# The down stage of eight feed-forward blocks: its units in another order

## What is computed

```python
def swiglu(h, w1, w3, w2):
    return (jax.nn.silu(h @ w1) * (h @ w3)) @ w2
# x = x + 0.5 * swiglu(rmsnorm(x, g), w1, w3, w2)   D = 1024, D_FF = 2816
```

## Time and profile before

| | us |
|---|---|
| median of 3 runs | 2255.55 |
| lowest, highest | 2254.95, 2256.36 |
| the profiled execution, its own time | 2255.33 |
| its span, first to last instruction | 2253.5 |
| TensorE busy | 2226.4 (99%) |
| TensorE weight loads | 1890.5 (84%) |
| VectorE busy | 1711.6 (76%) |
| ScalarE busy | 1305.8 (58%) |
| granted TensorE clock, mean | 1.000 (2.4 GHz) |
| DMA | 467.92 MB, 208 GB/s on average |

### The profile page before, as it was taken

One profiled execution on the slowest core, in us unless ns is written; L12 is line 12 of the kernel. 1 busy time (PEld: TensorE's weight loads), 2 busy tenths in 40 slices (PEclk: granted clock), 3 DMA queues, 4 the chain that ended last, 5 costly groups with the idle time before them and its releaser, 6 DMA issues.

```text
span 2253.5 us, 28616 instructions
## 1 busy us (share of the span) xinstructions
PE 2226.4 (99%) x11542; PEld 1890.5 (84%) x11542; DVE 1711.6 (76%) x2067; ACT 1305.8 (58%) x1425; POOL 42.2 (2%) x52
## 2 busy tenths in 40 slices
PE   9999999999999999999999999999999999999999
PEld 8888888888887888887888888888888878888887
DVE  7876567868878566877887799768788777976876
ACT  7655445555655544655655676455565557754654
POOL 0000000000000000000000000000000000000000
PEclk9999999999999999999999999999999999999999
DMA  7876455767758455577576753547667575345756
GB/s 264 261 225 245 168 191 181 249 199 229 233 181 278 171 178 196 200 226 237 206 245 213 235 171 128 205 157 244 216 225 238 169 254 200 107 168 196 232 181 204
DMA packets 171859, 467.92 MB, mean 208 GB/s; under 512 B 18608, under 2 KB 22576, under 8 KB 171728
## 3 DMA queue, kind: packets, MB, share of 16 engines
q1 hardware_dynamic: 164672, 428.35, 53.8%
q0 software_dynamic: 6912, 37.75, 9.3%
q10 hardware_dynamic: 144, 0.00, 0.0%
HBM read 464.99 MB, written 1.05 MB: 207 GB/s over the span
## 4 chain that ended last, share of the span: by engine, by line
PE 87%; DVE 9%; DMA 2%; ACT 1%; issue 0%; SPq 0%; DVEq 0%; ACTq 0%
PE psum L771 25%; PE psum L772 13%; PE psum L707 12%; PE psum L709 12%; PE psum L708 12%; DVE split_w L1851 4%; PE psum L782 3%; PE psum L739 2%; PE psum L790 2%; DVE split_w L1858 1%; DVE x L2048 1%; DVE late_sums L1867 1%; PE psum L900 1%; PE psum L904 1%; PE psum L902 1%; DMA raw<-ffn_w_down_alone_dram 1%
## 5 line engine op out<-in xcount | busy, mean ns | idle before, releaser
L1851 DVE TENSOR_TENSOR split_w<-raw,split_w 128x2048 fp32r<-128x2048 f32 (+2 forms) x405 | 854.1, 2118 | 179.6 <-ACT split_w L1328 177.6
L771 PE MATMUL psum<-xt,split_w 128*128 128x512 f32 x2464 | 858.7, 393 | 0.5 <-DVE split_w L1851 0.5
L1328 ACT ACTIVATE split_w<-raw 128x2048 fp32r<-128x2048 f32 (+2 forms) x405 | 716.7, 1778 | 204.6 <-PE psum L709 95.2
L772 PE MATMUL psum<-xt,split_w 128*128 128x256 f32 x2464 | 688.1, 279 | 0.0
L771 PEld LDWEIGHTS psum<-xt,split_w 128*128 128x128 f32 x2464 | 461.3, 187 | 105.2 <-DVE split_w L1851 2.2
L772 PEld LDWEIGHTS psum<-xt,split_w 128*128 128x128 f32 x2464 | 464.9, 189 | 0.3
L707 PE MATMUL psum<-split_w,xt 128*128 128x512 f32 (+1 forms) x736 | 289.5, 393 | 0.0
L709 PE MATMUL psum<-split_w,xt 128*128 128x512 f32 (+1 forms) x736 | 283.7, 385 | 0.0
L708 PE MATMUL psum<-split_w,xt 128*128 128x512 f32 (+1 forms) x736 | 283.6, 385 | 0.0
L1997 DVE TENSOR_TENSOR gate_up<-psum,low 128x512 f32<-128x512 f32 x176 | 121.0, 688 | 144.1 <-ACT low L1403 144.1
L1403 ACT ACTIVATE low<-psum 128x512 f32<-128x512 f32 x176 | 104.1, 591 | 173.8 <-PE psum L772 158.3
(11 more groups left out here) (305 smaller groups left out, 2839.2 us busy)
## 6 DMA issues: line engine op xcount, KB each, us to landing
raw<-w_in_dram SPq DMA_DIRECT2D x180, 512.0 KB, 4.4
raw<-t_gate_up_1b_dram SPq DMA_DIRECT2D x88, 512.0 KB, 4.7
raw<-t_gate_up_2a_dram SPq DMA_DIRECT2D x88, 512.0 KB, 4.7
raw<-t_gate_up_2b_dram SPq DMA_DIRECT2D x88, 512.0 KB, 4.7
raw<-t_gate_up_1a_dram SPq DMA_DIRECT2D x84, 512.0 KB, 4.8
early_sums<-ffn_w_down_quarters_dram POOLq DMA_DIRECT2D x24, 768.0 KB, 7.3
raw<-ffn_w_down_quarters_dram SPq DMA_DIRECT2D x48, 384.0 KB, 4.5
raw<-ffn_w_down_alone_dram SPq DMA_DIRECT2D x32, 512.0 KB, 7.1
```

Of the source, the lines that this page charges most:

```text
L771: nc.tensor.matmul(bank, whi[:, slot, w], xt[:, c, :, :], start=c == 0, stop=False)
L772: last = nc.tensor.matmul(bank[:, 0:T], wlo[:, slot, w], xt_hi[:, c, :], start=False, stop=c == DC - 1)
L1328: nc.scalar.activation(whi[:, e.unit(u) % HL, 0:n], raw[:, r, 0:n], ACT.Copy).then_inc(hi_done, 1)
L1851: nc.vector.tensor_tensor(wlo[:, e.unit(u) % HL, 0:n], raw[:, r, 0:n], whi[:, e.unit(u) % HL, 0:n], ALU.subtract).then_inc(w_ready, 1)
```

## The change

```diff
--- before.py
+++ after.py
@@ -52,9 +52,9 @@
     return tuple((kind, name, s) for s in range(SUPER))
 
 
-DOWN = ((("plain", 0, 0),) + each("sum", "U") + each("quarter", "11") + each("quarter", "21") + (("plain", 0, 1),)
-        + each("sum", "T2") + each("quarter", "22") + (("plain", 0, 2),) + each("sum", "T3") + each("sum", "T4")
-        + tuple(("plain", 1, i) for i in range(3)))
+DOWN = ((("plain", 0, 0),) + each("sum", "U") + each("quarter", "11") + (("plain", 0, 1),)
+        + (("sum", "T2", 0), ("quarter", "21", 0), ("sum", "T2", 1), ("quarter", "21", 1), ("plain", 0, 2),) + each("quarter", "22")
+        + each("sum", "T3") + (("plain", 1, 0),) + each("sum", "T4") + (("plain", 1, 1), ("plain", 1, 2)))
 AT = {part: i for i, part in enumerate(DOWN)}
 ADDED = {"T2": "22", "T4": "21"}
 BY_VECTOR = ('T3',)
@@ -885,11 +885,11 @@
                        "U": (BOTH, True, True), "21": (pair(2, 0), False, False), "T4": (pair(2, 1), False, True),
                        "22": (pair(1, 0), True, False)}
 
-                def products(name):
+                def products(name, groups=range(SUPER)):
 
                     out, start, stop = OUT[name]
                     resumed = name in ("T2", "T3")
-                    for s in range(SUPER):
+                    for s in groups:
                         u = u0 + 2 * FG + AT["quarter" if name in QUARTERS else "sum", name, s]
                         slot = e.unit(u) % HL
                         eng.wait_ge(w_ready, units(e, u, RAW))
@@ -914,25 +914,26 @@
                 eng.wait_ge(pair_free, ffn_blocks(e, f, FC - 1))
                 products("U")
                 products("11")
-                products("21")
                 eng.wait_ge(ht_done, ffn_pairs(e, f, 9))
                 alone(0, 1, False, False)
                 eng.wait_ge(taken, 2 * ffns(e, f) + 1)
-                products("T2")
-                products("22")
+                for s in range(SUPER):
+                    products("T2", (s,))
+                    products("21", (s,))
                 eng.wait_ge(ht_done, ffn_pairs(e, f, 10))
                 alone(0, 2, False, (True, False))
+                products("22")
                 eng.wait_ge(taken, 2 * ffns(e, f) + 2)
                 products("T3")
+                alone(1, 0, (False, True), False)
                 products("T4")
 
-                u = u0 + 2 * FG + AT["plain", 1, 0]
-                blocks(u, 0, 1, HT, ALONE[0][0:2], (False, True), False, False)
+                u = u0 + 2 * FG + AT["plain", 1, 1]
+                blocks(u, 0, 1, HT, ALONE[1][0:2], False, False, False)
                 if next_stage != "end":
                     eng.wait_ge(done, e.after(done, ("x", next_stage, 0)))
                     x_transposes(next_stage, 0)
-                blocks(u, 2, 1, HT, ALONE[0][2:4], False, False, True)
-                alone(1, 1, False, False)
+                blocks(u, 2, 1, HT, ALONE[1][2:4], False, False, True)
                 if next_stage == "end":
                     last_blocks(u0 + 2 * FG + AT["plain", 1, 2], 1, HT, ALONE[2])
                 else:
@@ -2105,45 +2106,41 @@
                 def used(i):
                     multiplied(u0 + 2 * FG + i)
 
-                def splits(kind, name):
-
-                    for s in range(SUPER):
-                        i = at(kind, name, s)
-                        added = [t for t, q in (("T2", "22"), ("T3", "22"), ("T4", "21")) if q == name and t in BY_VECTOR]
-                        for t in added:
-                            sum_added(u0 + 2 * FG + i, f, t, s)
-                        down_split(i)
-
-                splits("quarter", "11")
-                splits("quarter", "21")
+                for s in range(SUPER):
+                    down_split(at("quarter", "11", s))
                 down_split(at("plain", 0, 1))
                 used(at("quarter", "11"))
                 part_to_x(0, 0, EACH, rhalf).then_inc(taken, 1)
                 for m in range(MT):
                     part_to_x(m, 1, BOTH, rhalf)
-                splits("sum", "T2")
-                splits("quarter", "22")
+                for s in range(SUPER):
+                    down_split(at("sum", "T2", s))
+                    down_split(at("quarter", "21", s))
                 down_split(at("plain", 0, 2))
                 used(at("sum", "T2"))
-                split_before(at("plain", 0, 2))
+                split_before(at("sum", "T2"))
                 part_to_x(0, 1, EACH, minus_half).then_inc(taken, 1)
-                splits("sum", "T3")
-                splits("sum", "T4")
-                used(at("sum", "T3"))
-                split_before(at("sum", "T4"))
-                part_to_x(1, 0, EACH, rhalf)
-                part_to_x(1, 1, EACH, minus_half)
+                for s in range(SUPER):
+                    sum_added(u0 + 2 * FG + at("quarter", "22", s), f, "T3", s)
+                    down_split(at("quarter", "22", s))
+                for s in range(SUPER):
+                    down_split(at("sum", "T3", s))
+                down_split(at("plain", 1, 0))
+                for s in range(SUPER):
+                    down_split(at("sum", "T4", s))
                 used(at("plain", 0, 2))
                 part_to_x(0, 0, psum[:, 4, :], rhalf)
-                down_split(at("plain", 1, 0))
-                split_before(at("plain", 1, 0))
+                used(at("sum", "T3"))
+                part_to_x(1, 0, EACH, rhalf)
+                split_before(at("sum", "T4"))
+                e.link(part_to_x(1, 1, EACH, minus_half))
+                down_split(at("plain", 1, 1))
                 used(at("sum", "T4"))
                 last = part_to_x(1, 0, psum[:, 5, :], rhalf)
                 if next_stage == "end":
                     last.then_inc(out_ready, MT)
                 else:
                     last.then_inc(done, e.mark(done, ("x", next_stage, 0)))
-                down_split(at("plain", 1, 1))
                 down_split(at("plain", 1, 2))
                 if next_stage != "end":
                     x_lo(next_stage, 0)
```

## The result

The changed kernel takes 2289.22 us in the median of four runs (2286.69 to 2290.8) against 2255.55: a ratio of 1.0148, 95% interval 1.013 to 1.0166. It is 33.7 us slower. Its profiled execution took 2286.69, its span is 2284.9, 31.4 longer than before's. The forecast was 2272, so the sign was right and the size half of what came.

The account below looks back on a forecast made before the run. TensorE was busy 99% of the span, so only its waits for VectorE's splits could be won. Seven stages' 12.3, the fourth's -1.3 and the ends' 5.8 made 16.8 us on 2255.33: forecast 2272, range 2250 to 2290.

Parts of the forecast that it names:

- the clock: TensorE after a long wait: the clock might fall to 1.2 GHz, up to 7 us in all; not in the sum.
- 22/1: Down stages, behind 22/0: VectorE needs another 3.34 while TensorE has 2.15 of work, so 1.3 lost with restart.
- the mixing starts: Mixing stages behind down stages: first unit ready at 8.3 behind T4, wanted at 9.2, so nothing lost.
- What goes: Down stages: the losses at 21/1, P01 and P10 vanish; a stage loses 3.64 on average before, the eight 29.1 us.
- When things are issued: Down stage, from its first product: accumulating DMAs for T4 at +18.2 and +21.5, load of 22/0 at +19.3.
- 22/0, the main term: Down stages: 22/0's load, issued 1.1 behind an accumulating DMA, lands at +30.4; TensorE loses 4.0, and 0.1 behind it.
- packet for packet: DMA queues: 22/0's load and the accumulating pair alternate packets, so it ends about with the pair, 12.2 behind the first issue.
- The rival in between: Down stages: 22/0 is served between the two accumulations, there at +27.6, 2.6 lost a stage; 2253, chance 0.12.
- The fourth stage: Fourth down stage: SyncE's loads still flow, so 22/0 is served sooner; 2.6 lost against 3.9 before, -1.3.
- the rival "worse": Down stages: 22/0 held to the pair's end, lands at +32.2, 1.8 more in seven stages; 2285 and more, chance 0.15.
- The ends: Starts of the next stage: 1.4 each at two feed-forward starts, 3.0 more at the change of blocks; 5.8 in sum.

Follow-up runs that it names:

- hold21: Changed kernel with the accumulating DMAs for T4 held back until 21/0 (21/1) has been split: 2305.54 us, ratio 1.0219.
- holdP02: Changed kernel with both accumulating DMAs for T4 held back until P02 has been split: 2246.34 us, ratio 0.9955.
- hold22: Changed kernel with the accumulating DMAs for T4 held back until 22/0 (22/1) has been split: 2278.28 us, ratio 1.0096.
- holdP02_starts: holdP02 with feed-forward starts waiting for each weight unit by itself and, at the change of blocks, ScalarE squaring behind its next split: 2240.07 us, ratio 0.9927.
- pause2: holdP02_starts with VectorE repeating the subtraction of T3/0 twice more in every down stage: 2274.24 us, ratio 1.0078.
- pause2_filled: pause2 with 14 products that nobody reads put ahead of T3: 2262.03 us, ratio 1.0029.

## Why the prediction was half right

Which load would be late, and why, was right. The step that failed is the pricing of what follows from it. The sum put the clock at nothing, where it cost 8.1 us; it gave 22/1 only VectorE's work, 11.2, where it lost 15.8; and it gave the mixing starts nothing, where they lost 0.8. The terms follow one by one.

**What goes: right.** The waits at 21/1 and P01 are gone in all stages, and so is that at P10.

**When things are issued: right** to 0.1 us: +18.1 for 18.2, +21.5, +19.3.

**22/0, the main term: right in its mean, by luck in part, and wrong in its rule.** Predicted: landing at +30.4 and 4.0 lost in seven stages, some 1.3 in the fourth, 29.3 in all. Measured: a mean landing of +30.2 and 30.2 lost. But the landing isn't the one number of my "packet for packet": it goes from +28.0 to +32.6. DMA packets by queue in 153:157 and 157:160 of the first stage, beside the earlier trace rows:

```profile
q0 software_dynamic: 98, 0.50, 63.0%
q1 hardware_dynamic: 184, 0.52, 37.2%
...
q0 software_dynamic: 63, 0.39, 67.1%
q1 hardware_dynamic: 134, 0.36, 36.0%
```

Here two packets of 3 KB pass for each one of 6 KB, equal bytes, where before's P10 load with its 4 KB packets got about one for one. The rival in between had 22/0 landing at +27.6. The Trainium skill (DMA: Bandwidth & Descriptors, Queues, rings and completion order) has each engine go round its rings by whole groups of descriptors. The trace agrees in that both queues' packets pass in the same stretches (98 and 184, 63 and 134); the groups it doesn't show. What the rival made of it, a turn between the two accumulations, came true by half. The first half of 22/0 landed at +26.0, just behind the first accumulation (+25.6; so in seven stages, while in the sixth it was 0.9 ahead). The second half landed inside the second accumulation, or, in the third and sixth stages, with its end.

**The fourth stage: wrong, 4.4 us.** I expected its load to be served sooner, since SyncE's earlier loads were still flowing. DMA packets by queue in the first 4.9 us behind GpSimd's first issue, first stage (149.5:154.4), then fourth (1054.1:1059):

```profile
q0 software_dynamic: 92, 0.57, 64.9%
q1 hardware_dynamic: 284, 0.76, 39.5%
...
q1 hardware_dynamic: 487, 1.30, 68.2%
q0 software_dynamic: 61, 0.37, 37.2%
```

They did flow, 1.30 MB against 0.76, but these were the loads ahead of 22/0 in the same queue, and they held up the first accumulation too (0.37 MB against 0.57): it landed at +27.0 for +25.6, and 22/0 at +31.9. The stage is 3.1 longer, not 1.3 shorter. That this traffic made 22/0 late isn't shown, since in the third and sixth stages, without `gfin`, it landed as late or later.

**22/1: too small.** I gave it the 1.3 of VectorE's work. Its own load is issued at +22.7, behind the second accumulation, and in the first, fifth and eighth stages it landed too late even for VectorE (the idle 1.53 above). The eight stages lose 15.8 at 22/1, restarts counted (1.4 in each of five, and 3.0, 3.3 and 2.4 in these three), in place of 8 x 1.3 and 0.8 for restarts, 11.2.

**The clock: in the wrong place.** It stood in the rival "worse" with at most 7 us, at a chance of 0.15; it belonged in the sum. Its own cost is 5.4 in the stages, where much of the lower clock lies beneath 22/1's wait, and it also fell where I had not looked, at the change of blocks. Nine products at that level cost 1.8 more (0.43 apart for 0.23), not the 2.04 that I worked with.

**The ends: 5.8 predicted, 10.0 measured.** The two feed-forward starts cost 1.7 each for 1.4. That at the change of blocks waits 3.9 where before lost 0.7, so 3.1 more for the 3.0 predicted:

```profile
1103.74 0.79 PE L771 MATMUL psum<-xt,split_w 128*128 128x512 f32 x1 [3.73 <-DVE split_w L1852]
1104.33 0.41 PE L772 MATMUL psum<-xt,split_w 128*128 128x256 f32 x1
```

and 2.7 come on top, with the clock at 0.50 for 6.8 us (6.8 x 0.43 = 2.9). The mixing starts lose 0.1 to 0.35 where I had nothing, 0.8 in four.

**The books.** Profiled executions: 2286.69 against 2272.1 predicted for it, 14.6 missing. The stages are 10.0 of it: 0.9 at 22/0 (in it the fourth stage's error, set off by the others, which lost less), 4.6 at 22/1 and 5.4 for the clock make 10.9, which is 0.9 too much; this rest of the readings isn't placed. The ends are 4.2, of which 2.7 are the clock. 0.4 lie ahead of the first stage. Of the 14.6 the clock is 8.1. The median of the changed kernel is 2.5 above its profiled run, the lowest of the four, and what those 2.5 consist of no trace shows.

Left open: why 22/0's landing varies by 4.6 us between stages that issue the same transfers at the same times; why a load issued 0.5 us ahead of an accumulation was nearly left alone in hold21 (22/0) and held up in holdP02 (P10's); and why equal waits of 3.1 us brought the clock down in five stages and not in three. A hold of one accumulation and not of the other wasn't tried.

## What to carry to other kernels

When an order is changed, list every load against every accumulating DMA, by issue time, before and after. 22/0 landed 4.6 to 9.1 us later for being issued 1.1 us behind one (the changed kernel against hold22, stage by stage). Holding the accumulation back until the loads that are wanted first are under way costs one wait on GpSimd, and won 43 us here. Follow the held transfer to its own consumer, and look at the load next to it, since the lateness has to go somewhere with slack. And price a new wait of TensorE of 2 us or more at more than itself: where the clock falls, add 0.43 us for each us of lower clock that no other wait covers.

## What the hardware showed that I had not expected

- **A wait can cost more than itself.** Equal waits of 3.1 us on TensorE were followed by 3.4 or 6.8 us at 1.2 GHz in five cases of eight; those of 1.4 in none; 14 products in the wait's place kept 2.4 GHz. The 2.1 at P11 in hold22 was followed by it in five of eight, single waits of 2.2 (before) and 2.5 (holdP02_starts) were not. The Trainium skill says that a gate between clock source and array passes half or all of the pulses according to how busy TensorE has been (TensorE: Matmul & The Clock Gate, What's actually happening). The pair pause2 and pause2_filled agrees, with 12.2 us between them. The Trainium skill, the same page (HAM oscillation — how this bites in real kernels), counts half of the time at the lower level as lost; measured is 0.43 of it. That equal waits had unequal effects is measured here.
- **Queues share neither by turns of one packet nor by order of issue.** 47 packets of 4 KB went beside 54 of 6 KB, and 184 of 3 KB beside 98 of 6 KB.
- **Half a microsecond ahead can save a load, but need not.** In hold21 22/0 was issued 0.5 us ahead of the accumulation and landed 4.8 to 6.0 after its issue (4.1 to 5.2 in hold22, with no accumulation near). In the changed kernel, issued 1.1 behind it, it took 8.7 to 13.3. P10's load in holdP02, of 512 KB a half and also issued 0.5 ahead, took 10.2 to 13.1 against 6.0 to 7.6.
